# Key heads turned in pairs by transpose and copied between row halves by on-chip transfers, key stacks ahead of query stacks

## What is computed

```python
k_slc = rope_partial(k_slc, pos)            
k_win = rope_partial(k_win, pos)            
s = einsum('bqhgd,bhqnld->bhgqnl', qblk, k_g)      # selected
p_slc = softmax(where(m, s, -1e30))
s = einsum('bqhgd,bkhd->bhgqk', qblk, kw)          # window
p_win = softmax(where(mw, s, -1e30))
o = g[..., 0:1] * o_cmp + g[..., 1:2] * o_slc + g[..., 2:3] * o_win
```

## Time and profile before

| | |
|---|---|
| median of 3 runs | 864.59 us (864.23 to 864.84) |
| profiled execution, its time | 864.83 us |
| its span in the trace | 863.0 us |
| busy: TensorE | 825.7 us (96%) |
| busy: VectorE | 536.1 us (62%) |
| busy: ScalarE | 457.0 us (53%) |
| busy: POOL | 375.9 us (44%) |
| chain that ended last | TensorE 75%, VectorE 13%, ScalarE 7% |

### The profile page before, as it was taken

One profiled execution on the slowest core, in us unless ns is written; L12 is line 12 of the kernel. 1 busy time (PEld: TensorE's weight loads), 2 busy tenths in 40 slices (PEclk: granted clock), 3 DMA queues, 4 the chain that ended last, 5 costly groups with the idle time before them and its releaser, 6 DMA issues.

```text
span 863.0 us, 12472 instructions
## 1 busy us (share of the span) xinstructions
PE 825.7 (96%) x4642; PEld 688.3 (80%) x4642; DVE 536.1 (62%) x940; ACT 457.0 (53%) x931; POOL 375.9 (44%) x331
## 2 busy tenths in 40 slices
PE   8999999999999999999899999999989999999995
PEld 7878788888888788786788877788768888887884
DVE  2762349861762706467999999999973044463435
ACT  4604154222333015658899998889874252625424
POOL 3302118235131120745446666456635445463554
PEclk9999999999999999999999999999999999999999
DMA  9501011101111010320000000000019523232327
GB/s 303 120 28 49 25 36 48 49 26 49 26 49 49 14 49 24 97 83 1 1 2 2 1 2 1 2 2 0 2 36 320 180 86 98 76 107 74 98 94 248
DMA packets 38158, 55.19 MB, mean 64 GB/s; under 512 B 11073, under 2 KB 17489, under 8 KB 38098
## 3 DMA queue, kind: packets, MB, share of 16 engines
q1 hardware_dynamic: 37810, 53.34, 20.2%
q0 software_dynamic: 288, 1.05, 0.7%
HBM read 49.13 MB, written 5.25 MB: 63 GB/s over the span
## 4 chain that ended last, share of the span: by engine, by line
PE 75%; DVE 13%; ACT 7%; issue 3%; POOL 2%; DMA 0%; DVEq 0%; SPq 0%; ACTq 0%; POOLq 0%
PE psum L928 47%; PE psum L1215 3%; DVE pT_lo L2183 3%; PE psum L1043 3%; DVE p_slc L2155 3%; ACT pT_hi L1572 2%; PE psum L954 2%; PE psum L1193 2%; PE psum L1238 1%; PE psum L1194 1%; PE psum L1239 1%; PE psum L849 1%; PE psum L851 1%; PE psum L850 1%; DVE o_sum L2195 1%
## 5 line engine op out<-in xcount | busy, mean ns | idle before, releaser
L1694 POOL TENSOR_TENSOR w_lo<-w_raw,w_hi 128x512 fp32r<-128x512 f32 x126 | 179.7, 1430 | 339.5 <-ACT w_hi L1346 339.0
L1346 ACT ACTIVATE w_hi<-w_raw 128x512 fp32r<-128x512 f32 x126 | 79.5, 635 | 315.3 <-PE psum L928 293.1
L928 PE MATMUL psum<-w_hi,xT_hi 128*128 128x512 f32 x256 | 101.1, 395 | 1.7 <-DVE gla_state_b L2060 1.7
L928 PE MATMUL psum<-w_hi,xT_lo 128*128 128x512 f32 x256 | 99.7, 390 | 0.0
L928 PE MATMUL psum<-w_lo,xT_hi 128*128 128x512 f32 x256 | 99.7, 389 | 0.0
L2183 DVE TENSOR_TENSOR pT_lo<-psum,pT_hi 128x512 fp32r<-128x512 f32 (+1 forms) x148 | 93.0, 655 | 9.0 <-ACT pT_hi L1572 8.1
L1572 ACT ACTIVATE pT_hi<-psum 128x512 fp32r<-128x512 f32 (+1 forms) x148 | 80.8, 569 | 15.4 <-PE psum L1215 13.2
L1193 PE MATMUL psum<-kT,qT_hi_lo 128*128 128x384 f32 (+3 forms) x192 | 65.5, 345 | 3.3 <-DVE neg_max L2155 2.9
L1750 POOL TENSOR_SCALAR p_slc<-p_slc,gate_over_sum 128x512 f32<-128x512 f32 (+7 forms) x40 | 65.4, 1646 | 1.6
L1194 PE MATMUL psum<-kT,qT_hi_lo 128*128 128x384 f32 (+3 forms) x192 | 60.7, 329 | 0.0
L1238 PE MATMUL psum<-pT_hi,v_hi_lo 128*128 128x512 f32 x132 | 59.7, 452 | 0.6 <-DVE pT_lo L2183 0.5
(11 more groups left out here) (290 smaller groups left out, 1982.1 us busy)
## 6 DMA issues: line engine op xcount, KB each, us to landing
w_raw<-in_w_in SPq DMA_DIRECT2D x56, 256.0 KB, 2.7
w_raw<-in_w_out SPq DMA_DIRECT2D x32, 256.0 KB, 2.7
w_raw<-in_ple_gate SPq DMA_DIRECT2D x32, 256.0 KB, 2.6
x_tok<-in_x SPq DMA_DIRECT2D x8, 512.0 KB, 8.2
h_tok<-in_x SPq DMA_DIRECT2D x8, 512.0 KB, 6.2
out<-h_tok SPq DMA_DIRECT2D x6, 512.0 KB, 5.5
w_raw<-in_ple_proj SPq DMA_DIRECT2D x8, 256.0 KB, 2.6
cmp_w<-in_cmp_w_k SPq DMA_DIRECT2D x16, 64.0 KB, 2.1
```

Of the source, the lines that this page charges most:

```text
L928: mm = pe.matmul(out, lhs, rhs, start=(first and n == 0), stop=(final and n == 2))
L1346: act.activation(w_hi(i)[:, 0:w], w_in(i)[:, 0:w], ACT.Copy).then_inc(s_whi, 1)
L1694: pool.tensor_tensor(w_lo(i)[:, 0:w], w_in(i)[:, 0:w], w_hi(i)[:, 0:w].bitcast(F32), ALU.subtract).then_inc(s_wlo, 1)
```

## The change

Two key heads that lie side by side in the token layout (the two of one branch) are turned by one set of four transposes, as two query heads are; the odd head of the pair lands in rows 64 to 127 and the even one in rows 0 to 63, and both are rounded by one operation on each engine, into the odd head's table. SP then copies within the chip, after the rounding: the even head into both halves of its own table (`even_keys`, two transfers of 64 rows x 2 x 512), and, once these have landed, the odd head from rows 64 to 127 into rows 0 to 63 (`odd_keys`, one transfer). There are twelve transfers in all. The key stacks go to the front of `stacks`, which has 13 entries instead of 17, and `soon` becomes 10. The wait of the mask table becomes `s_qtr >= 6` and moves from behind piece 4 to behind piece 6. The planner gets a job for each pair's copies (3200 ns, on queues of their own) and the scores depend on it.

```diff
-        return KT[:, h % 2 * 2 + h // 2, 0]
+        return KT[:, h, 0]
...
+    s_kcopy = [[sem(f"keys_copied_{pair}_{half}") for half in range(2)] for pair in range(2)]
...
-    stacks = [("q", h, 0) for h in range(4)] + [("c", 0, 0)] + [("k", h, 0) for h in (0, 2, 1, 3)] \
-        + [("q", 0, 1), ("k", 0, 1), ("q", 1, 1), ("k", 2, 1), ("q", 2, 1), ("k", 1, 1), ("q", 3, 1), ("k", 3, 1)]
-    first_half, soon = 9, 13
-    stack_bank = [4, 5, 0, 2, 4, 5, 4, 5, 4] + [5, 4, 5, 4] + [1, 3, 1, 3]
-    stack_piece = {9: 1, 10: 1, 11: 3, 12: 3}
+    stacks = [("k", 0, 0), ("k", 1, 0)] + [("q", h, 0) for h in range(4)] + [("c", 0, 0)] \
+        + [("q", 0, 1), ("k", 0, 1), ("q", 1, 1), ("k", 1, 1), ("q", 2, 1), ("q", 3, 1)]
+    soon = 10
+    stack_bank = [4, 5, 0, 2, 4, 5, 4] + [5, 4, 5] + [1, 3, 1]
+    stack_piece = {7: 1, 8: 3, 9: 3}
...
+    def keys_needed(step):
+
+        kv, qt, br = step
+        return [(br - 1, half) for half in range(1 + (qt >= NT // 2))] if br else []
...
-            ops["stack_turn", u] = "P", {"q": 600, "k": 1100, "c": 450}[kind], late
+            ops["stack_turn", u] = "P", {"q": 600, "k": 600, "c": 450}[kind], late
...
+            if kind == "k":
+                pair = stacks[u][1]
+                ops["key_copy", 2 * half + pair] = f"D{2 * half + pair}", 3200, 0
+                after["key_copy", 2 * half + pair] = [("stack_lo", u)]
...
+        def even_keys(pair, half):
+
+            cols = slice(half * 512, half * 512 + 512)
+            sp.wait_ge(s_qlo, stacks.index(("k", pair, half)) + 1)
+            for r in (slice(0, 64), slice(64, 128)):
+                sp.dma_start(KT[r, 2 * pair, :, cols].bitcast(F32),
+                             KT[0:64, 2 * pair + 1, :, cols].bitcast(F32)).then_inc(s_kcopy[pair][half], 16)
+
+        def odd_keys(pair, half):
+
+            cols = slice(half * 512, half * 512 + 512)
+            sp.wait_ge(s_kcopy[pair][half], 32)
+            sp.dma_start(KT[0:64, 2 * pair + 1, :, cols].bitcast(F32),
+                         KT[64:128, 2 * pair + 1, :, cols].bitcast(F32)).then_inc(s_kcopy[pair][half], 16)
...
             if i == piece0[cidx["nzB"]] + 4:
-                sp.wait_ge(s_qtr, 4)
+                even_keys(0, 0)
+                even_keys(1, 0)
+            if i == piece0[cidx["nzB"]] + 6:
+                sp.wait_ge(s_qtr, 6)
                 sp.dma_start(MK[:], a["masks"]).then_inc(s_mk, 16)
+        odd_keys(0, 0)
+        odd_keys(1, 0)
+        for pair in range(2):
+            even_keys(pair, 1)
+        for pair in range(2):
+            odd_keys(pair, 1)
...
-                    for r in (slice(0, 64), slice(64, 128)):
-                        mm = pe.matmul(bank(stack_bank[u])[r, i * P:(i + 1) * P], KSW[:, t, h], ident,
-                                       start=True, stop=True)
+                    mm = pe.transpose(bank(stack_bank[u])[:, i * P:(i + 1) * P],
+                                      KSW[:, t, 2 * h:2 * h + 2].rearrange("p h d -> p (h d)"), ident)
...
+                for pair, half in keys_needed(steps[s]):
+                    if (kv, pair, half) not in keys_there:
+                        keys_there.add((kv, pair, half))
+                        pe.wait_ge(s_kcopy[pair][half], 48 if kv else 32)
...
-                ins = act.activation(k_hi(h)[:, cols], ps, ACT.Copy)
+                ins = act.activation(k_hi(2 * h + 1)[:, cols], ps, ACT.Copy)
...
-                ins = dve.tensor_tensor(k_lo(h)[:, cols], ps, k_hi(h)[:, cols].bitcast(F32), ALU.subtract)
+                ins = dve.tensor_tensor(k_lo(2 * h + 1)[:, cols], ps, k_hi(2 * h + 1)[:, cols].bitcast(F32), ALU.subtract)
```

More of the change, by code:

```diff
@@ L180, in k_hi @@
     def k_hi(h):
-        return KT[:, h % 2 * 2 + h // 2, 0]
+        return KT[:, h, 0]
     def k_lo(h):
-        return KT[:, h % 2 * 2 + h // 2, 1]
+        return KT[:, h, 1]
     VC = sm("vc_hi_lo", [P, NKV, 2, P], F32R)
@@ L579, in stacks_needed @@
         if qt >= NT // 2:
-            return len(stacks) if kv else soon
-        last = [("q", 2 * kv + 1, 0), ("c", 0, 0) if br == 0 else ("k", (br - 1) * NKV + kv, 0)]
-        return max(stacks.index(x) for x in last) + 1
+            return len(stacks)
+        need = [("q", 2 * kv + 1, 0), ("c", 0, 0) if br == 0 else ("k", br - 1, 0)]
+        return max(stacks.index(x) for x in need) + 1
+    def keys_needed(step):
+        kv, qt, br = step
+        return [(br - 1, half) for half in range(1 + (qt >= NT // 2))] if br else []
     def attention_timeline():
@@ L639, in attention_timeline @@
                 ops["score", n] = "P", 0.86 * nk + 290, s
-                after["score", n] = after_pair(pair_freed(s, g)) + [("stack_lo", stacks_needed(step) - 1)]
+                after["score", n] = after_pair(pair_freed(s, g)) + [("stack_lo", stacks_needed(step) - 1)] \
+                    + [("key_copy", 2 * half + pair) for pair, half in keys_needed(step)]
                 ops["mask_max", n] = "V", 1.04 * nk + 158, s
@@ L670, in attention_timeline @@
                  "exponent", "csum", "mask_max", "cscore", "score", "gate_z", "gate_mul", "first_mul", "gate_sig", "stack_lo", "stack_hi", "stack_turn",
-                 "gate_lo", "gate_hi", "gate_mm", "gate_end"]
-        overlap = {"P": 162, "V": 83, "A": 103, "G": 28}
+                 "gate_lo", "gate_hi", "gate_mm", "gate_end", "key_copy"]
+        overlap = {"P": 162, "V": 83, "A": 103, "G": 28, "D0": 0, "D1": 0, "D2": 0, "D3": 0}
         hand = {"PV": 37, "PA": 36, "VP": 55, "AP": 55, "GP": 80, "AV": 32, "VA": 35, "VG": 80, "AG": 80, "GV": 60, "GA": 60}
@@ L690, in attention_timeline @@
         queue = {k: sorted(n for kind, n in ops if kind == k) for k in kinds}
-        free, end, line = {"P": 0, "V": 3000, "A": 3000, "G": 0}, {}, []
+        free, end, line = {"P": 0, "V": 3000, "A": 3000, "G": 0, "D0": 0, "D1": 0, "D2": 0, "D3": 0}, {}, []
         while len(line) < len(ops):
@@ L1178, in compressed_scores @@
             mm.then_inc(s_cqk, 1)
+        keys_there = set()
         def scores(n):
```

## The result

The changed kernel takes **869.52 us** (median of 4 runs, 869.02 to 871.2), against 864.71 for the kernel before on the same chip: a ratio of 1.006, with a 95% interval of 1.0048 to 1.0072. It is 4.8 us slower, where 867.1 stood as the forecast: the right side and the stall that was named, at about twice the size. The profiled execution took 869.76 us, with a span of 867.7.

A forecast was written before the change was run, and what follows sets the result against it. VectorE was taken to bound attention, TensorE close behind: idle time 16.8 + 1.0 - 12.7 = +5.1 us and work -2.6 us give +2.5 us on the median of 864.59, so 867.1 us, range 861.8 to 870.8.

The forecast's parts named there:

- The stall, 4.8 us: Start of attention: TensorE stands from 386.3 to 391.1 us for piece 7, the last gate weights, queued behind the mask table.
- VectorE's gap, 16.8 us: Start of attention: VectorE has nothing from 374.1 to 390.9 us, until the queries' low parts; 16.8 us idle.
- Idle time after 391 us, 1.0 us: VectorE's further idle time once the queries' low parts start: 1.0 us taken, 0 to 4 us allowed.
- Work, -2.6 us: Start of attention: key rounding falls from 8 to 4 pairs of operations, so VectorE loses 2.6 us of work.
- The sum, +2.5 us: VectorE's account at the start of attention: +5.1 us idle, -2.6 us work; +2.5 us, with +1.5 to +5.5 allowed.
- The clock: After the stall TensorE's clock falls to 0.50, losing 1.7 us on column blocks 0 and 1; about 0.5 us comes through.
- The copies, nothing: On-chip key copies at the start of attention land before the first score needs them, after 394 us; cost nothing.
- TensorE is the bound after all: Rival: in attention TensorE's own sum counts, -4.0 us, giving 860.6 us; chance 0.18.
- Colder and longer: Rival: ScalarE sets the pace after 394 us and the clock stays low through blocks 2 and 3; +6, 870.6 us; chance 0.12.
- The copies hold: Rival: first four copies land at 401 us, 6 us after the first score could start; +6 to +8, 872; chance 0.04.
- it cancels: Rival: reordered attention changes the 9.8 us idle by 2 or 3 us, or piece 7 lands sooner; 864.6 us; chance 0.26.

The follow-up runs named there:

- e4: The changed kernel with the twelve copies and the waits on them left out: 870.43 us.
- e10: The e9 kernel with the mask table's wait and load moved behind the load of piece 7: 868.07 us.
- e6: The e1 kernel with the twelve copies and the waits for them left out: 864.03 us.
- e3: The changed kernel with eleven matmuls that add zero placed in TensorE's stall before piece 7: 869.33 us.
- e2: The changed kernel with key stacks behind the queries and compressed keys, the mask table loaded behind piece 7 and the first copies behind the table: 861.29 us.
- e8: The e5 kernel with each set of key pair transposes done four times: 861.72 us.
- e5: The changed kernel with two query turns planned ahead of gate piece 1 and two ahead of piece 2: 858.94 us.
- e7: The e5 kernel with each key rounding done twice on ScalarE and VectorE: 862.86 us.
- e1: The changed kernel with the load of piece 7 issued ahead of the mask table's wait: 863.28 us.
- e9: The kernel before, first query turn forced behind gate piece 4 and the mask table's wait moved behind piece 6's load, without pairing or copies: 877.11 us.

## Why the forecast came out on the right side at half the size

- **The stall, 4.8 us:** right. Key turns from 368.55, the queries' turns at 383.05, the table at 384.99 and piece 7 at 385.36 (385.0 and 385.4 were given), TensorE idle for 5.24 us until 391.58. Landing took 4.2 us, not 3.7; the odd heads' copies, issued 0.5 us behind it, were new beside it, and without them it took 3.4 (e4).
- **VectorE's gap, 16.8 us:** 15.11. It ended at 391.30 instead of 390.9, but began at 376.2 instead of 374.1: three multiplications were put at 0.62 us each and took 1.33 on average. That did not help, for it is time moved from idle to busy.
- **Idle time after 391 us, 1.0 us:** this step failed in size: it was put at 1.0 us and measured 3.0. It was the term with the widest bounds. VectorE idled 1.0 us from its restart to 402 us (2.29 in the stretch, less 1.30 up to 391.30), 1.8 from 402 to 420 and 0.3 to 430: 3.0 us, within the 0 to 4 that was given. Its longest piece is the gap in VectorE's timeline below, behind a first turn that had waited for a query stack. TensorE's granted clock was 0.50 again from 413 to 416 us, after a wait of 1.50 us; the sum had no term for that. New score work did not come faster than VectorE took it, though following its queue had told me that it would. Its idle time from 374 to 430 us rose by 5.4 us (5.1 forecast), since the shorter gap and this term nearly cancel; that this part of the sum came out so well is luck.

```profile
415.84 0.56 DVE L2195 CUSTOM_DVE_ANT_0 p_slc<-psum,masks 128x384 f32<-128x384 f32 x1 [1.03 <-PE psum L1234]
```

- **Work, -2.6 us:** the roundings fell by 2.7, but the multiplications gave back 1.1, a cost for which the forecast had no term. Their groups over the attention stretch, before and after:

```profile
L2096 DVE TENSOR_TENSOR nsa_zT<-nsa_zT,sigmoid_tmp 128x512 f32<-128x512 f32 x8 | 6.5, 865 | 0.0
```
```profile
L2136 DVE TENSOR_TENSOR nsa_zT<-nsa_zT,sigmoid_tmp 128x512 f32<-128x512 f32 x8 | 7.6, 981 | 0.0
```

- **The sum, +2.5 us:** the median rose by 4.8 and the span by 4.7. The stretch grew by 3.8, that is 1.1 for the multiplications and 0.3 of idle time above the forecast (rounding takes up the rest). The other 0.9 us of the span lie outside it. What stands behind the stretch (span less the time of the GLA turn) is the same work in every version, yet took from 220.3 us (e10) to 224.2 (e6); 220.6 before and 221.2 after are inside that spread, and no run ties the difference to the change.
- **The clock:** the low stretch came as forecast, over by 396 us, and these 1 us stretches answer to the earlier trace rows; e3 could not find its 0.5 us (0.2 by the medians), and can't exclude it either. The wait for the key stack of the earlier trace rows went, as forecast, and one of 1.5 us for a query stack took its place (the last line, from the waits of 402 to 430 us):

```profile
391.00:392.00 1.00, 0.42 (x1) 0.42 (x2) 0.69 (x1) 0.96 (x3) 0.52 (x1) 0.50 0.00 0
...
399.00:400.00 1.00, 1.00 (x9) 0.83 (x7) 0.77 (x2) 0.72 (x2) 0.00 (x0) 1.00 0.00 0
...
PE psum L1250 <- DVE qT_hi_lo L2149: 1.5, 1, 1.5
```

- **The copies, nothing:** right for the time, by e4 and e6, though they made the stall 0.7 us longer. It is a matter of the order: in e2, where they go out late, the first score waits 1.03 us for them.
- **The rivals:** "TensorE is the bound after all" fell for this kernel, yet e8 found about half of the price of its work real, and e5 landed in the range of the same rival. The forecast gave TensorE's 6.3 us no worth by themselves; that was wrong as soon as the stall was away. "Colder and longer" fell by its own test (VectorE idled 1.4 us from 396 to 410 us, not over 3) and by the clock, which was 1.00 again from 396 us; ScalarE was indeed full from 402 to 410 us, 7.9 of 8 us, but not from 396 (12.1 of 14). "The copies hold" fell with e4 for this order. For "it cancels": VectorE's idle time behind 430 us in the stretch was 13.53 us before (212.43 less 198.90) and 13.55 after (216.49 less 202.94), so nothing cancelled there.

## What to carry to other kernels

When a change moves a job behind others, look in every hand-written queue for a wait on that job, and ask what stands behind the wait: here one line that kept a small table's load ahead of the last weights cost 6.2 us, about as much as the saved work was worth (5.8 to 6.7 us by e7 and e8). Judge such a change in two parts, work and order, by running the order alone in the old kernel; here the new order, with the queries' turns behind five gate pieces, hid a gain of 5.2 us. Where TensorE stood because another engine was late, keeping its clock up with filler bought nothing that could be measured. And where the profile names an engine as what ended a wait, look whether the wait needs that engine's work: in e2 it was a copy.

## What the hardware showed that I had not expected

**Multiplications beside POOL.** VectorE's multiplication of two on-chip tables, 128x512, took 0.67 us alone, and 1.68 and 1.78 when it began while one of POOL's low parts was under way; each ended 0.55 us after POOL's. POOL's took 1.26 us alone, and 1.74 and 1.49 when they began during a multiplication; each ended 1.15 us after it. The one that began first kept its time (0.68 us for the third multiplication, 1.29 for the low part at 372.05), so the later one waits for the earlier to end. The same stands in the traces of e1, e2, e5 and e9. The operations of VectorE that read one operand from PSUM kept their 0.68 to 0.69 us beside POOL too. The Trainium skill says why ("SBUF — State Buffer", "Who interferes with whom"): a VectorE instruction with two SBUF inputs contends with a GpSimd instruction that reads SBUF. The trace agrees.

**Transfers within the chip.** The copies moved 205 GB/s from 374 to 378 us, with the transfer engines busy 0.98 of the time, while 379 to 380 us, with the loads of pieces 5 and 6, shows 318 (stretches of the changed kernel; the last three columns are PEclk, share and GB/s):

```profile
374.00:378.00 4.00, 4.00 (x19) 3.34 (x18) 2.19 (x2) 0.63 (x1) 2.53 (x2) 1.00 0.98 205
379.00:380.00 1.00, 1.00 (x6) 0.84 (x5) 0.00 (x0) 0.04 (x1) 0.00 (x0) 1.00 0.84 318
```

The Trainium skill ("SBUF — State Buffer", "Door 1: The DMA port swizzle") says that 64 partitions reach 8 of 16 ports. The rates agree with it, but no copy of 128 rows was run, so this case does not show that the ports are the reason; the time of the changed kernel does not depend on it.
